# Bank rotation, halo copy, roots and tile order at the seams of an eight-core encoder kernel

## The reference

```python
def layer(x, pool_buf, conv_buf, ffn_buf, offset, ...):
    h = rmsnorm(x, g_pre_mix)
    z = h @ w_in                                  # [v | B | C | u], 512 columns each
    v, gb, gc, u = split(z)
    pooled = multiscale_pool(v, pool_buf)         # trailing means of 2, 4, 8, 16 tokens minus v
    ya = per_group_matmul(pooled, pool_mix) * pool_scale
    yb = gb * causal_dwconv(gc * u, conv_w)       # 3 taps
    mix = concat(head_rmsnorm(ya), head_rmsnorm(yb)) @ w_out
    x = x + rmsnorm(mix, g_post_mix)
    h = rmsnorm(x, g_pre_ffn)
    up = causal_dwconv(h @ w_up, ffn_conv_w)      # 2 x 2816 columns, 3 taps
    f = (silu(up[..., :D_FF]) * up[..., D_FF:]) @ w_down
    return x + rmsnorm(f, g_post_ffn)
```

## Time and profile before

| | |
|---|---|
| median of 3 runs | 2847.02 us (the lowest 2844.59) |
| the profiled execution's own time | 2846.09 us |
| its span, slowest core (core 5) | 2844.6 us |
| spans of the eight cores | 2833.7 to 2844.6 us |
| mean granted TensorE clock by core | 0.989 to 0.991 |
| TensorE busy | 2706.2 us (95%) |
| VectorE, ScalarE, GpSimd busy | 1939.2, 1503.4, 1050.2 us |
| the chain that ended last | TensorE 80%, VectorE 8%, ScalarE 4% |

### The profile page before, as it was taken

One profiled execution on the slowest core, in us unless ns is written; L12 is line 12 of the kernel. 1 busy time (PEld: TensorE's weight loads), 2 busy tenths in 40 slices (PEclk: granted clock), 3 DMA queues, 4 the chain that ended last, 5 costly groups with the idle time before them and its releaser, 6 DMA issues.

```text
span 2844.6 us, 44614 instructions; the slowest of 8 cores (2833.7 to 2844.6 us)
## 1 busy us (share of the span) xinstructions
PE 2706.2 (95%) x13984; PEld 1365.3 (48%) x13984; DVE 1939.2 (68%) x2355; ACT 1503.4 (53%) x2713; POOL 1050.2 (37%) x1077
## 2 busy tenths in 40 slices
PE   6999999999999999999889999999999999998998
PEld 2444444444444444444446645456454565455653
DVE  5877367864787467865678836688457885478863
ACT  5754365544754356545665535655356554475543
POOL 3444054431544144530544304444135432254320
PEclk9999999999999999999999999999999999999999
DMA  7684274733574265746547425474244843347421
GB/s 161 97 144 80 39 126 92 126 63 71 97 141 83 47 114 105 130 74 159 100 88 117 73 32 109 85 118 68 45 91 75 138 71 52 73 82 135 71 44 64
DMA packets 195255, 261.78 MB, mean 92 GB/s; under 512 B 138576, under 2 KB 139984, under 8 KB 195024
## 3 DMA queue, kind: packets, MB, share of 16 engines
q0 software_dynamic: 52992, 189.82, 40.3%
q1 hardware_dynamic: 142032, 69.11, 10.7%
HBM read 406.88 MB, written 9.29 MB: 146 GB/s over the span
## 4 chain that ended last, share of the span: by engine, by line
PE 80%; DVE 8%; ACT 4%; issue 4%; DMA 2%; POOL 1%; SPq 1%; DVEq 0%; ACTq 0%; POOLq 0%
PE psum_all L366 80%; DVE sb_r L400 3%; ACT sb_r L384 2%; DVE sb_r L389 2%; DVE sb_r L427 1%; DVE sb_hs L400 1%; ACT sb_tp L538 1%; ACT sb_r L424 1%; DMA sb_h<-sb_hs 1%; DMA sb_x<-xp 1%; SPq L605 1%; DVE sb_tp L400 1%; POOL sb_r L389 0%; DMA sb_g<-gains 0%; ACT sb_ss L384 0%
## 5 line engine op out<-in xcount | busy, mean ns | idle before, releaser
L366 PE MATMUL psum_all<-sb_h,sb_w 128*128 128x370 bf16 (+2 forms) x9600 | 1788.4, 347 | 55.6 <-DVE sb_r L427 26.5
L366 PEld LDWEIGHTS psum_all<-sb_h,sb_w 128*128 128x128 bf16 x9600 | 941.5, 99 | 868.0 <-issue 105.8
L389 POOL TENSOR_TENSOR sb_r<-sb_r 128x1104 bf16<-128x1104 f32 (+13 forms) x428 | 664.1, 1552 | 958.8 <-PE psum_all L366 336.2
L366 PE MATMUL psum_all<-sb_w,sb_r 128*128 128x512 bf16 (+1 forms) x4080 | 887.6, 379 | 0.0
L366 PEld LDWEIGHTS psum_all<-sb_w,sb_r 128*128 128x128 bf16 (+1 forms) x4080 | 400.8, 99 | 479.2 <-issue 6.7
L427 DVE SCALAR_TENSOR_TENSOR sb_r<-psum_all,sb_vec,sb_r 128x736 f32<-128x736 f32 (+1 forms) x704 | 542.9, 790 | 85.9 <-PE psum_all L366 36.1
L400 DVE SCALAR_TENSOR_TENSOR sb_r<-psum_all,sb_vec,sb_r 128x1023 f32<-128x1023 f32 (+3 forms) x432 | 463.0, 1083 | 136.4 <-ACT sb_r L384 77.4
L384 ACT ACTIVATE sb_r<-psum_all,sb_vec 128x1024 f32<-128x1024 f32 (+4 forms) x368 | 288.0, 813 | 262.6 <-PE psum_all L366 231.1
L424 ACT ACTIVATE sb_r<-psum_all,sb_vec 128x736 f32<-128x736 f32 (+1 forms) x352 | 253.8, 722 | 298.1 <-PE psum_all L366 297.5
L442 POOL DMA_DIRECT2D sb_w<-wts x360 | 206.5, 575 | 484.7 <-PE psum_all L366 460.1
L400 DVE SCALAR_TENSOR_TENSOR sb_tp<-psum_all,sb_ss,sb_g 128x1024 f32<-128x1024 f32 x136 | 174.2, 1282 | 309.6 <-ACT sb_ss L384 254.1
(11 more groups left out here) (52 smaller groups left out, 563.8 us busy)
## 6 DMA issues: line engine op xcount, KB each, us to landing
sb_w<-wts POOLq DMA_DIRECT2D x360, 512.0 KB, 6.4
sb_g<-gains SPq DMA_DIRECT2D x33, 512.0 KB, 4.7
sb_x<-xp SPq DMA_DIRECT2D x16, 512.0 KB, 6.8
yp<-sb_x SPq DMA_DIRECT2D x9, 512.0 KB, 2.7
yp<-sb_r SPq DMA_DIRECT2D x7, 512.0 KB, 2.9
sb_h<-sb_hs SPq DMA_TRANSPOSE x128, 3.1
sb_pm<-pm POOLq DMA_DIRECT2D x8, 128.0 KB, 4.5
sb_tp<-gains SPq DMA_DIRECT2D x1, 512.0 KB, 7.0
```

The costliest lines, as they stand in the source:

```text
L366: P.op(PE, lambda h: h.matmul(oa, la, ra, start=start, stop=stop), reads=[lv.r(llo, lhi), rv.r(rlo, rhi)], writes=[ov.r(olo, ohi)])
L389: P.op(eng, lambda h: h.tensor_tensor(oa, aa, ba, op), reads=[av.r(alo, ahi), bv.r(blo, bhi)], writes=[ov.r(olo, ohi)])
```

## The change

Six edits, in the order of the diff:

- In the first layer's first slot the fourth projection (`bb`) is issued ahead of the turns of tiles 4 to 7, and all four tiles are turned in one run, ahead of `a_ca` and `d_taps`; before, tiles 4 and 5 were turned ahead of these, and 6 and 7 behind the fourth projection.
- For the last tile of w_out, the post-norm's root is made alone, and the tile two before has a `pre_tile` of its own behind the post-norm.
- Part 1 of `up_b` takes its single bank from all eight, not from 6 and 7.
- In the second block's lead, bank pairs are taken as they are needed, and the order on TensorE is k = 0 of q0, q1, q2, then k = 1 of q0, k = 0 of q3, k = 1 of q1, q2, q3 (`c0`, `c1`); the two pre-norms stay ahead of the convolutions of q0 and q2.
- In the first block the halo copy is issued behind part 1 of the leads.
- In the second block the deferred pre-norm of the last tile moves from slot 0 to slot 1 of the next layer's mixer.

```diff
--- before.py
+++ after.py
@@ -873,9 +873,12 @@
                         m.d_pooled()
                     if first and si == 0:
 
+                        m.bb = mm_bank()
+                        z_mm(m.c, m.bb, j, 1, 1)
                         turn = Turn("pre", range(2, 4))
-                        for t in tiles[4:6]:
+                        for t in tiles[4:]:
                             turn.push(t)
+                        turn.flush()
                     m.a_ca()
                     do(p1, "a_rstd")
                     m.d_taps()
@@ -884,13 +887,10 @@
                         f[0]()
                     for f in now:
                         f[1]()
-                    m.bb = mm_bank()
-                    z_mm(m.c, m.bb, j, 1, 1)
+                    if not (first and si == 0):
+                        m.bb = mm_bank()
+                        z_mm(m.c, m.bb, j, 1, 1)
                     issue_weights(pace[si])
-                    if first and si == 0:
-                        for t in tiles[6:]:
-                            turn.push(t)
-                        turn.flush()
                     if ci == NCH - 1:
                         for (_, q) in zu.pop(j):
                             release(q)
@@ -960,11 +960,13 @@
                     rs.square((bankpair[pk].rows(t["p"]), 0, D), t["p"])
 
                     t2 = tiles[ti - 2] if ti >= 2 and ti != urgent + 2 else None
-                    if t2 is not None:
+                    if t2 is not None and ti < len(tiles) - 1:
                         rs.square((xt(t2), 0, D), t2["p"])
                     rs.root()
                     post_apply(t, pk, DVE if ti in own_adds else POOL, rs.col(0))
-                    if t2 is not None:
+                    if ti == len(tiles) - 1:
+                        pre_tile(t2, "pre")
+                    elif t2 is not None:
                         pre_apply(t2, "pre", rs.col(1))
                     if ti == urgent + 1:
                         pre_tile(tiles[urgent], "pre")
@@ -1082,7 +1084,7 @@
                             conv_b(fv, 0, 2, 2 * pk, jt)
                         if part != 0:
                             k = 2 if part == 2 else k0
-                            bk = take_bank((6, 7) if k == 2 else range(6))
+                            bk = take_bank((6, 7) if part == 2 else range(8))
                             u_mm(ws, t_, banks[bk], HO - 2 + k * KN, KN + 2)
                             conv_b(fv, k, 1, bk, jt)
                         fs.append(fv)
@@ -1097,25 +1099,32 @@
                         gates.append(up(i, lead[i][0], 0, gated=False))
                         pre_tile(tiles[i - 2], "pre")
                         issue_weights(1)
-                    hh = b_hh.t[:, l * KT:l * KT + KT].bitcast(BF16).rearrange("p (k c) -> p k c", k=KT)
-                    hl = h3[:, :, HO + 1022:HO + 1024]
-                    P.op(POOL, lambda h, o_=hh, i_=hl: h.tensor_copy(o_, i_), reads=[hv[kt].r(HO + 1022, HO + 1024) for kt in range(KT)],
-                         writes=[(b_hh, l * KT, l * KT + KT)])
                 else:
 
-                    pks = [take_pair(range(4)) for _ in range(4)]
-                    for q in range(4):
+                    pks = []
+
+                    def c0(q):
+                        pks.append(take_pair(range(4)))
                         u_mm(lead[q // 2][0], q % 2, banks[2 * pks[q]], HO - 2, KN + 2)
-                    for i in range(2):
-                        pre_tile(tiles[i - 2], "pre")
-                        fs = []
-                        for t_ in range(2):
-                            b0 = 2 * pks[2 * i + t_]
-                            u_mm(lead[i][0], t_, banks[b0 + 1], HO - 2 + KN, KN + 2)
-                            fs.append(next_fa())
-                            conv_b(fs[-1], 0, 2, b0, i + NPAIR * t_)
-                        gates.append(lambda i=i, fs=fs: gate(i, fs[0], fs[1], 0, 2 * KN))
-                        issue_weights(1)
+
+                    def c1(q):
+                        b0 = 2 * pks[q]
+                        u_mm(lead[q // 2][0], q % 2, banks[b0 + 1], HO - 2 + KN, KN + 2)
+                        fv = next_fa()
+                        conv_b(fv, 0, 2, b0, q // 2 + NPAIR * (q % 2))
+                        return fv
+
+                    for q in range(3):
+                        c0(q)
+                    pre_tile(tiles[-2], "pre")
+                    fs = [c1(0)]
+                    c0(3)
+                    fs.append(c1(1))
+                    issue_weights(1)
+                    pre_tile(tiles[-1], "pre")
+                    fs += [c1(2), c1(3)]
+                    issue_weights(1)
+                    gates += [lambda i=i: gate(i, fs[2 * i], fs[2 * i + 1], 0, 2 * KN) for i in range(2)]
                 for g in gates:
                     g()
                 for i in range(2, nlead):
@@ -1128,6 +1137,11 @@
                     up(i, lead[i][0], 1)
                     release(lead[i][1])
                     issue_weights(2)
+                if bi == 0:
+                    hh = b_hh.t[:, l * KT:l * KT + KT].bitcast(BF16).rearrange("p (k c) -> p k c", k=KT)
+                    hl = h3[:, :, HO + 1022:HO + 1024]
+                    P.op(POOL, lambda h, o_=hh, i_=hl: h.tensor_copy(o_, i_), reads=[hv[kt].r(HO + 1022, HO + 1024) for kt in range(KT)],
+                         writes=[(b_hh, l * KT, l * KT + KT)])
                 for i in range(nlead, NPAIR):
                     ws, wq = next_unit("u")
                     up(i, ws, 2)
@@ -1166,7 +1180,7 @@
                     elif last_layer:
                         final_tile(t, "pre")
                     elif last:
-                        deferred = [[later(t, "pre")]]
+                        deferred = [[] for _ in range(bi)] + [[later(t, "pre")]]
                     else:
                         pre_tile(t, "pre")
                     if last:
```

## The result

The changed kernel took 0.9927 of the time before (95% interval 0.9898 to 0.9955), about 2825 us against 2846: a gain of some 21 us. It is under two per cent, though the interval leaves out 1. Forecast were 2822 us, a ratio of 0.9916 to those 2846. In some runs the cores of one die show a lower granted clock and a longer time; such runs are left out of every comparison here. The profiled execution has a span of 2822.8 us on its slowest core (core 7), against 2844.6; TensorE's busy time, for the same matmuls, is 10 us less, and its idle time makes the rest. Of the 10 us some 7 are clock (core 5 lost 30.3 us to it before, core 7 loses 23.2), and I put the rest to the drain that ends each run of matmuls: TensorE stops for over 0.1 us in 92 places instead of 115.

What follows compares the result with a forecast made beforehand. TensorE was taken as the bound, busy 2706.2 of 2844.6 us, so only idle and low-clock time could be won. 2846.1 - 25 - 3.5 + 4.5 - 0.5 = 2821.6, predicted 2822 us, range 2808 to 2838.

Steps and rivals of the forecast that it cites:

- Lead pairs, -25: Second block's lead stages: gains of 26.3 us over four layers, taken as -25; bounds -14 and -33.
- 5.0 us a layer for the two-bank rotation: Second block's lead singles: the rotation costs TensorE 5.0 us in layer 2; with eight banks singles 3 to 8 don't stop.
- layer 1's 8.4: Second block's layer 1 lead stage: gains 8.4 us from the 40.6 us it takes.
- 2.6 + 0.2 drain + 1.6 of clock + 5.0 removed: Layer 1's lead: wait at the joint root, drain, low clock and bank rotation go; 1.0 put back, gain 8.4 us.
- for which I had 6.4: Second block's layer 0 lead stage: credited 6.4 us, 1.4 of it for matmuls at the lower clock.
- I cost both at nothing: Second block's leads, layers 0, 2 and 3: reordering and the last tile's root alone gain nothing; VectorE's order is unchanged.
- Halo copy, -3.5: First block: copy behind part 1 waits for nothing, 0.9 us a layer, -3.5 us; bounds -4.5 and +3.
- The rival by which GpSimd holds VectorE out: First block: GpSimd's multiplication delays the last tile's scaling and transpose 2 us in four layers; 2834 us, 6%.
- Slot 1, +4.5: Second block's mixers, layers 1 to 3: moving the last tile's pre-norm to slot 1 loses +1.5 us a layer.
- the bound of +14: Upper bound for the slot 1 move: each new wait is followed by a low-clock stretch.
- Initial tiles, -0.5: Kernel's start: some 0.5 of ScalarE's 0.72 us scaling leaves the turns' chain, -0.5 us; bounds -1.7 and +3.
- The slower rival: Second block's up projection: VectorE sets the pace, its backlog stays and the down projection waits; 2850 us, 6%.

Runs made afterwards that it cites:

- e1: The kernel before with one edit, the second block's single lead tiles take any of eight banks; 0.9916 of before, -24 us.
- e11: As e9, without the order, root, halo and start edits (eight banks and split pre-norm alone); 0.9878 of before, median 2809.2 us.
- e6: On e5, the last tile's pre-norm split: scaling and transposes go one slot later, behind that slot's gate, in both blocks; 0.9870 of before.
- e9: On e6, last tile's output and sample tile's load moved to the first slot at the second block's start; 0.9862 of before, median 2804.8 us.
- e10: As e9, but the sample tile's pre-norm is not split; 0.9877 of before, median 1.9 us above e9.
- e12: The changed kernel with unused matmuls ahead of the two waiting matmuls in the second block's mixers of layers 1 to 3; 0.9909 of before.
- e5: The changed kernel with the last tile's deferred pre-norm back in the mixer's first slot in the second block; 0.9898 of before, median 2824 us.
- e2: The kernel before with only the second block's lead chunks reordered and bank pairs taken as wanted; one timed run, 2870.71 us, no ratio.
- e7: The kernel before with only the first block's halo copy issued behind the lead's second part; 0.9976 of before (0.9945 to 1.0007).
- e4: The kernel before with only the second block's deferred last-tile pre-norm moved to the mixer's second slot; 1.0035 of before, about 10 us slower.

## Why the prediction was right

**Lead pairs, -25: right, -26.1.** The 5.0 us a layer for the two-bank rotation was right: 19.2 us of full time in four layers against 20, and the same 19.4 from the banks alone. Beyond it I had credited 6.3 us, 4.5 of them clock and 1.8 layer 1's wait, less 1.3 that might return; 6.9 were measured, all of it clock, within the scatter named above.

Within the term, layer 1's 8.4 was too much: its up projection fell by 6.3 us (median of the cores). Its root alone is indeed done by the time the sample tile's square begins. The step that failed is the 2.6 in "2.6 + 0.2 drain + 1.6 of clock + 5.0 removed", the whole wait put down to the joint root: 1.42 us of it stay, which are VectorE's queue, as in the other layers. ScalarE's, VectorE's and TensorE's timelines after, in layer 1:

```profile
1822.54 0.20 ACT L384 ACTIVATE sb_ss<-sb_ss 128x1 f32<-128x1 f32 x1
1822.64 1.04 ACT L538 ACTIVATE sb_tp<-sb_x 64x1024 fp8e5<-64x1024 f32 x1
...
1818.84 4.59 DVE L400 SCALAR_TENSOR_TENSOR sb_hs<-sb_x,sb_ss,sb_g 128x1024 bf16<-128x1024 f32 x2
1823.36 2.46 DVE L400 SCALAR_TENSOR_TENSOR sb_tp<-psum_all,sb_ss,sb_g 128x1024 f32<-128x1024 f32 x2
...
1824.77 1.41 PE L366 MATMUL psum_all<-sb_h,sb_w 128*128 128x370 bf16 x8 [1.42 <-DVE sb_tp L400]
```

The two scalings that hold the queue run beside an add of GpSimd, as in rows 5, and take 2.1 us more than the two behind them, which is more than the wait; no run tests what it would be without that add. And the 1.6 of clock in layer 1's term were read from core 5; the mean over the cores is 0.85. Layer 0's 7.7, for which I had 6.4, made up for it.

"I cost both at nothing" for the order and the root holds in full time. For the clock it is open: with the banks and without these two, 2.1 (e1) and 4.1 us (e11) are lost in these stages, with all three 0.2 to 0.9 in five kernels (after, e6, e9, e10, e12) but 3.2 in e5. Together they turn waits of 1.42 and 2.26 us into 1.42, 0.63 and 1.45; in e2 the order alone does so in layers 0, 2 and 3, but layer 1, without its own root, keeps one of 2.51. That this division holds the clock is argued from five of these six kernels, and e5 speaks against it; no kernel has the banks with just one of the two.

**Halo copy, -3.5: right in mechanism, -4.0 in full time** (means 610.8 with the new place, 614.8 with the old), and 2 to 3 once the clock is counted (e7's timing alone cannot tell). The changed kernel's profile shows 2.3 full (2.4 with clock), because the last tile's transpose landed late on several of its cores. VectorE's 0.36 us waits of TensorE are gone, and the wait for the transpose stays on some of the cores, as said. The rival by which GpSimd holds VectorE out went the way I expected. Timeline after, the two engines at the last tile's scaling in the first block's layer 1:

```profile
470.18 2.18 POOL L389 TENSOR_TENSOR sb_r<-sb_r 128x512 bf16<-128x512 f32 x1 [0.34 <-DVE sb_r L400]
...
469.95 1.27 DVE L400 SCALAR_TENSOR_TENSOR sb_hs<-sb_x,sb_ss,sb_g 128x1024 bf16<-128x1024 f32 x1
```

The scaling issued first and took its normal time; the multiplication, 1.27 us elsewhere, took 2.18. This agrees with the rule that I cited from the Trainium skill ("SBUF — State Buffer", Who interferes with whom): the later to issue waits.

**Slot 1, +4.5: right sign and mechanism, too small: +6.9.** By the table 4.8 of it is full time, close to the term, and 2.1 is clock, which I put into the bound of +14 and not into the term; e4 alone showed 8.1, 4.3 and 3.8. I forecast waits of 1.5 and about 3; they are 1.97 and, at full clock, 3.57. That some of the growth is clock is shown by e12; that it is 2.1 is not, since one execution scatters more than that.

**Initial tiles, -0.5: nothing.** In the kernels with this edit the start takes 92.8 to 94.3 us full, in those without 94.4 to 95.6, about 1.5 less; but they lose 3.8 us or more to the clock instead of 2.1 to 2.8. The low clock that I allowed for in the bound takes it all.

**The slower rival** did not come about: the second block's down projections have the same length to 0.02 us in every kernel (median of the cores), with eight banks as with two, so VectorE has no backlog at the end of the stage.

The sum held because three misses were small and of both signs: lead -1.1, slot 1 +2.4, the halo as seen in this profile +1.1. That is partly luck: each of them holds lost clock, which in a single execution can be several us more or less.

## What to carry to other kernels

If an engine rotates through too few buffers, count what the slower neighbour needs per buffer against what the faster one needs: the price of the rotation can be read from one timeline, and idle buffers give all of it back if the neighbour catches up later. A stall that can't be removed may still be worth dividing: 3.2 us in one piece cost more on the average than 1.6 and 1.05 in two places, because TensorE kept its clock. And before moving a step from one slot to the next, ask which half of it must move: here the root could stay, and the scaling needed to go behind the next gate, which turned a loss of 7 us into a gain of about 6.

## What the runs showed of the hardware

How much of TensorE's time depends on how its waiting is spread. In the mixers of layers 1 to 3 the granted clock was 1.00 throughout in the four kernels that split the pre-norm (e6, e9, e10, e11: 90 mixers), with a wait of 1.60 to 1.88 us and one of 1.05 to 1.34 near it. With waits of 1.97 and then 1.98 to 3.57 us, in the changed kernel, it fell to 0.50 at or behind them in each of 24 mixers. With matmuls of no use in these waits it did not fall at all (e12). A single wait does not decide it: with one of 3.17 to 3.46 us, before, it fell in 16 of 24 mixers and stayed at 1.00 in 8, seven of them in layer 2, the mixer of rows 9. The windows of before over the mixers of layers 1 and 2 (columns as in rows 6):

```profile
1718.90:1796.00 77.10, 69.95 (x419) 40.80 (x418) 52.73 (x84) 51.31 (x97) 40.46 (x68) 0.96 0.56 103
2091.80:2165.60 73.80, 66.90 (x418) 39.65 (x417) 53.13 (x84) 51.20 (x97) 40.50 (x68) 1.00 0.60 108
```

What decides between the two is not shown here. Over the whole kernel 29.2 us are lost to the clock before, 24.0 after and 16.6 in e9: of the 40 us that e9 gained, about 13 are clock.
